# Feed-forward of a hybrid layer: two output tiles accumulated together, in two PSUM banks in turn

## The reference

```python
D_MODEL = 1024; SEQ = 2048; D_FF = 4 * D_MODEL
mix = hybrid_mixer(x, mem, ...)
x = layer_norm(alpha * x + mix, ln1_g, ln1_b)
ff = jnp.square(jax.nn.relu(x @ w_ff1)) @ w_ff2
x = layer_norm(alpha * x + ff, ln2_g, ln2_b)
```

## Time and profile before

| | |
|---|---|
| Median of 3 runs | 2450.43 us (2450.17 to 2451.43) |
| Span of the profiled execution | 2450.3 us |
| PE busy | 2343.9 us, 96% |
| DVE busy | 1361.9 us, 56% |
| ACT busy | 758.7 us, 31% |
| POOL busy | 345.0 us, 14% |
| Matmuls | 10560 |

### The profile page before, as it was taken

One profiled execution on the slowest core, in us unless ns is written; L12 is line 12 of the kernel. 1 busy time (PEld: TensorE's weight loads), 2 busy tenths in 40 slices (PEclk: granted clock), 3 DMA queues, 4 the chain that ended last, 5 costly groups with the idle time before them and its releaser, 6 DMA issues.

```text
span 2450.3 us, 29301 instructions
## 1 busy us (share of the span) xinstructions
PE 2343.9 (96%) x10560; PEld 1880.9 (77%) x10560; DVE 1361.9 (56%) x2145; ACT 758.7 (31%) x1242; POOL 345.0 (14%) x261
## 2 busy tenths in 40 slices
PE   7999999998999997999999999998999999999996
PEld 5777777777778776788888888886788888888885
DVE  4666558555846577544454454447755454454456
ACT  4434443453444344321211212215421211212213
POOL 3221112110211137200000000004720000000003
PEclk9999999999999998999999999999999999999998
DMA  6223241324132323411111111111211111111111
GB/s 182 61 58 106 61 155 35 107 66 138 49 107 69 121 90 133 155 47 50 40 51 51 34 51 51 39 47 35 93 65 49 51 51 51 34 51 51 35 51 69
DMA packets 171279, 174.17 MB, mean 71 GB/s; under 512 B 5520, under 2 KB 139696, under 8 KB 171200
## 3 DMA queue, kind: packets, MB, share of 16 engines
q1 hardware_dynamic: 160256, 134.23, 18.2%
q0 software_dynamic: 10944, 38.91, 4.3%
HBM read 156.35 MB, written 16.78 MB: 71 GB/s over the span
## 4 chain that ended last, share of the span: by engine, by line
PE 57%; DVE 5%; DMA 0%; ACT 0%; issue 0%; SPq 0%
PE main L67 9%; PE main L69 9%; PE main L68 9%; PE sc L67 5%; PE sc L68 5%; PE sc L69 5%; PE ob L67 2%; PE aux L67 2%; PE aux L69 2%; PE ob L68 2%; PE aux L68 2%; PE ob L69 2%; DVE f_xT_lo L1386 2%; DVE f_stats L1635 1%; DVE acc L1629 1%; DMA acc<-normed_dram 0%
## 5 line engine op out<-in xcount | busy, mean ns | idle before, releaser
L1629 DVE TENSOR_TENSOR acc<-acc,main 128x512 f32<-128x512 f32 x512 | 347.3, 686 | 217.1 <-PE main L69 217.1
L67 PE MATMUL main<-w_lo,h_hi 128*128 128x512 f32 x1024 | 405.8, 396 | 3.9 <-issue 2.0
L69 PE MATMUL main<-w_hi,h_hi 128*128 128x512 f32 x1024 | 404.6, 395 | 0.0
L68 PE MATMUL main<-w_hi,h_lo 128*128 128x512 f32 x1024 | 404.3, 395 | 0.0
L1553 ACT ACTIVATE w_hi<-raw 128x1024 fp32r<-128x1024 f32 x124 | 124.1, 1049 | 538.2 <-PE main L69 538.2
L1015 DVE TENSOR_TENSOR w_lo<-raw,w_hi 128x1024 fp32r<-128x1024 f32 x120 | 159.5, 1336 | 163.9 <-ACT w_hi L742 162.3
L67 PEld LDWEIGHTS main<-w_lo,h_hi 128*128 128x128 f32 x1024 | 192.7, 188 | 49.5 <-issue 2.4
L69 PEld LDWEIGHTS main<-w_hi,h_hi 128*128 128x128 f32 x1024 | 192.6, 188 | 45.6
L68 PEld LDWEIGHTS main<-w_hi,h_lo 128*128 128x128 f32 x1024 | 192.7, 188 | 45.1
L67 PE MATMUL main<-xT_lo,w_hi 128*128 128x512 f32 (+1 forms) x528 | 219.4, 416 | 1.5 <-DVE xT_lo L1027 1.5
L67 PE MATMUL sc<-f_xT_lo,w_hi 128*128 128x512 f32 x512 | 204.0, 398 | 17.3 <-DVE f_xT_lo L1386 17.3
(11 more groups left out here) (207 smaller groups left out, 3989.6 us busy)
## 6 DMA issues: line engine op xcount, KB each, us to landing
raw<-in_w_ff_dram SPq DMA_DIRECT2D x128, 512.0 KB, 4.0
raw<-in_w_in_dram SPq DMA_DIRECT2D x80, 512.0 KB, 3.8
rows<-in_x_dram POOLq DMA_DIRECT2D x32, 512.0 KB, 5.1
raw<-in_w_out_dram SPq DMA_DIRECT2D x32, 512.0 KB, 4.0
normed_dram<-rows POOLq DMA_DIRECT2D x16, 512.0 KB, 3.3
out_dram<-acc POOLq DMA_DIRECT2D x12, 512.0 KB, 3.0
acc<-normed_dram SPq DMA_DIRECT2D x8, 512.0 KB, 11.9
acc<-normed_dram POOLq DMA_DIRECT2D x8, 512.0 KB, 7.0
```

The lines of the kernel that those rows point to most:

```text
L67: pe.matmul(dst, a_hi, b_lo, start=first, stop=False)
L68: pe.matmul(dst, a_lo, b_hi, start=False, stop=False)
L69: return pe.matmul(dst, a_hi, b_hi, start=False, stop=last)
L1629: dve.tensor_tensor(dst, dst, fo[i % 4][:, :], ALU.add).then_inc(fo_free[i % 4], 1)
```

## The change

In the feed-forward, two tiles are made at once by a new function `pair`: for each step of the sum it issues high x low for both tiles, then low x high for both, then high x high for both. `hidden` pairs the two feature groups of a token group (sc0 with sc1, ob with aux), `project` the two column halves of a row group (main0 with main1, main2 with main3). `project` now takes c, and waits for both banks before the pair's first matmul. The wait for slot 1 of the weights moves ahead of the first hidden tile. In (0, 15) two transposes now stand behind each pair. The programs of ACT, DVE, POOL and SP are not changed; the ends of two tiles (`fm_done`, `fo_done`) are now signalled by two matmuls in a row.

```diff
@@ -1489,41 +1489,56 @@
     def _(pe):
         three = three_products(pe)
 
+        def pair(first, second, count):
+
+            for n in range(count):
+                pieces = [side(n) for side in (first, second)]
+                for dst, a_hi, a_lo, b_hi, b_lo in pieces:
+                    pe.matmul(dst, a_hi, b_lo, start=n == 0, stop=False)
+                for dst, a_hi, a_lo, b_hi, b_lo in pieces:
+                    pe.matmul(dst, a_lo, b_hi, start=False, stop=False)
+                done = [pe.matmul(dst, a_hi, b_hi, start=False, stop=n == count - 1)
+                        for dst, a_hi, a_lo, b_hi, b_lo in pieces]
+            return done
+
         def hidden(hf, fb):
 
-            for i in range(4):
-                f, sb_ = i % 2, i // 2
-                if i < 2:
-                    pe.wait_ge(lo_done, slot_n(hf, fb, f) + 1)
+            for sb_ in range(2):
+                if sb_ == 0:
+                    pe.wait_ge(lo_done, slot_n(hf, fb, 1) + 1)
                 pe.wait_ge(hraw_ready, h_n(hf, fb, 0))
                 tok = slice(512 * sb_, 512 * sb_ + 512)
-                for k in range(KT):
-                    col = slice(P * k, P * k + P)
-                    ins = three(fm[i][:, :], w_hi[:, f, col], w_lo[:, f, col], xT_hi[:, k, tok], xT_lo[:, k, tok],
-                                k == 0, k == KT - 1)
-                ins.then_inc(fm_done, 1)
-
-        def project(hf, fb, i):
-
-            c, d = i // 2, i % 2
-            if i == 0:
+
+                def tile(f):
+                    return lambda k: (fm[2 * sb_ + f][:, :], w_hi[:, f, P * k:P * k + P], w_lo[:, f, P * k:P * k + P],
+                                      xT_hi[:, k, tok], xT_lo[:, k, tok])
+
+                for ins in pair(tile(0), tile(1), KT):
+                    ins.then_inc(fm_done, 1)
+
+        def project(hf, fb, c):
+
+            if c == 0:
                 pe.wait_ge(lo_done, slot_n(hf, fb, 3) + 1)
-            if i % 8 == 0:
-                pe.wait_ge(h_lo_ready, h_n(hf, fb, 2 + i // 4))
-            if isinstance(fb, int) and hf == 0 and fb == 0 and i < 4:
-                pe.wait_ge(ff.main_free[i], ff.first_slot // 4)
-            pe.wait_ge(fo_free[i % 4], 4 * NFB * hf + 4 * fb + i // 4)
+            if c % 4 == 0:
+                pe.wait_ge(h_lo_ready, h_n(hf, fb, 2 + c // 2))
+            for i in (2 * c, 2 * c + 1):
+                if isinstance(fb, int) and hf == 0 and fb == 0 and i < 4:
+                    pe.wait_ge(ff.main_free[i], ff.first_slot // 4)
+                pe.wait_ge(fo_free[i % 4], 4 * NFB * hf + 4 * fb + i // 4)
             tok = slice(P * c, P * c + P)
-            for f in range(2):
-                ins = three(fo[i % 4][:, :], h_hi[:, f, tok], h_lo[:, f, tok],
-                            w_hi[:, 2 + f, 512 * d:512 * d + 512], w_lo[:, 2 + f, 512 * d:512 * d + 512],
-                            f == 0, f == 1)
-            ins.then_inc(fo_done, 1)
+
+            def tile(d):
+                return lambda f: (fo[(2 * c + d) % 4][:, :], h_hi[:, f, tok], h_lo[:, f, tok],
+                                  w_hi[:, 2 + f, 512 * d:512 * d + 512], w_lo[:, 2 + f, 512 * d:512 * d + 512])
+
+            for ins in pair(tile(0), tile(1), 2):
+                ins.then_inc(fo_done, 1)
 
         def both(hf, fb):
             hidden(hf, fb)
-            for i in range(16):
-                project(hf, fb, i)
+            for c in range(8):
+                project(hf, fb, c)
 
         pe.wait_ge(x_lo_ready, 16)
         both(0, 0)
@@ -1531,7 +1546,8 @@
             both(0, fb)
         hidden(0, NFB - 1)
         for i in range(16):
-            project(0, NFB - 1, i)
+            if i % 2 == 0:
+                project(0, NFB - 1, i // 2)
             if i == 0:
                 pe.wait_ge(hraw_ready, h_n(1, 0, 0))
             transpose_rows(pe, ff, 1, i)
```

## The result

The changed kernel takes 2483.93 us (median of 4 runs, 2478.3 to 2486.13), the kernel before 2450.3 beside it (2450.1 to 2451.43): a ratio of 1.013, 95% interval 1.0113 to 1.0148. The forecast was 2478.4 with a range of 2464 to 2488.

What follows compares the result with a forecast made beforehand. TensorE, busy 96% of the span, was taken to bound the kernel. Terms 11.8 + 2.0 + 4.5 + 7.9 + 1.8 = 28.0 us on 2450.4 gave 2478.4 us, range 2464 to 2488.

Steps and rivals of the forecast that it cites:

- part 1 (two banks in turn): All feed-forward matmuls: alternating banks, or repeating a stationary tile, leaves the 233.3 ns step unchanged; taken as 0.
- the gain of 108 or 123 us: Feed-forward steps shorten by 17.6 ns (108 us) or 20 ns (123 us); the shorter-step rival, 2355 us, had 6%.
- a loss beyond those two values: Rival: opening another bank each time lengthens feed-forward steps by 1 to 3 ns, +6 to +18 us; 4%.
- a clock that gives way: Rival: cycling through PSUM banks drops the feed-forward to the lower clock, 1229 us more, about 3680 us; 1%.
- Part 2, the chain: End of a block's first layer: two tiles ready together make the second layer's first add 1.76 us late.
- The stall: Before the second layer's third pair, TensorE waits for two adds: 0.42 us a block, bounds 0.2 to 0.65.
- (1,1): Second half's second block: the regular 0.42 us stall, plus 2.0 us because h_lo can meet POOL once.
- The start of the feed-forward: Before and in the first block (0,0): hidden tiles are late anyway, so no loss; 0.
- (0,15): Boundary between halves: later chain and one more slow x_low, 4.5 us, or 1.8 if that one escapes.
- (1,0): Second half's first block, with statistics on DVE: 6.0 us later restart plus 1.9 us lower clock, 7.9 us.
- (1,15): Last block: DVE has no slack, so its late start goes straight to the end, 1.8 us.
- The 28 stalls: All blocks but four special ones: 28 x 0.42 = 11.8 us, bounds 5.6 to 18.2.

Runs made afterwards that it cites:

- e1: Changed kernel with only the first layer's hidden tiles in pairs, the second layer tile by tile as before: 2463.77 us, ratio 1.0053.
- e2: Kernel before with only the second layer's tiles in pairs, the hidden tiles one by one: 2456.84 us, ratio 1.0026.
- e4: Changed kernel with ACT and DVE ordered by kind for a pair (both relus, both h_raw, both h_hi, both h_lo): 2463.6 us, ratio 1.005.
- e8: Changed kernel with the edits of e3, e4 and e5, and POOL and statistics arranged as in e7: 2444.81 us, ratio 0.9971.
- e3: Changed kernel with the wait for the pair's second bank moved to just ahead of the pair's second matmul: 2476.53 us, ratio 1.0104.
- e6: Kernel before with POOL's scaling of the second half's rows held back until all x_low are done: 2445.38 us, ratio 0.9968.
- e7: e6 with five of the eight statistics of block (1,0) moved behind later adds: 2439.59 us, ratio 0.9947 against the kernel before.
- e5: Changed kernel with the first two hidden tiles of the first block made one after the other, each with its own weight wait: 2481.61 us, ratio 1.0119.
- e9: The kernel of e7 run once more beside e8 on the same chip: 2442.1 us, ratio 0.9959 against the kernel before.

## Why the prediction was right, and by how much it was off

**What bounds the kernel, and part 1 (two banks in turn): right.** I had taken 0 from the equal steps of the earlier trace rows, with a bound of 0.01 us a step. e1, e2, e4 and e8 have blocks of 44.61 or 44.79 us with one layer or both in pairs, and these are the two values of the kernel before. There is neither the gain of 108 or 123 us nor a loss beyond those two values, which are 1 ns a step apart, and the granted clock was 1.00 in the regular blocks of the changed kernel, against the rival of a clock that gives way. The two matmuls in a row with the same stationary tile bring nothing either.

**Part 2, the chain: right to 0.01 us.** 1.76 late was forecast, 4.58 us after the second layer's start; it is 4.59. **The stall: right in kind, sized too low.** 0.42 was forecast, 0.48 to 0.51 is what the blocks show. The step that failed is the hand-over taken from the earlier trace rows, 0.05 us from an add's end to the waiting matmul. Here the pair of adds (1547.90, 1.28 long) ends at 1549.18 and the matmul is recorded at 1549.32, 0.14 later. The two values are not scatter. Wherever a matmul was released by an add, the delay is 0.055 us in every kernel with one bank wait ahead of it (before, e1, e3, e6, e7, e8: 13 times), and 0.146 us in every kernel with two (the changed one, e2, e4, e5: 78 times). The row of the prediction was right for one wait, and the pair has two. Why the second costs 0.09 us is open. Together with the difference between the two halves below it makes 13.4 us for the 27 blocks besides (1,1), for 11.3: 2.1 of the 4.5 us that the sum was short.

**The start of the feed-forward: set to 0.** The prediction named (0,0) and set it to 0 since its hidden tiles are late in any case. It did not follow the moved wait for slot 1 to its first use, where DVE is still at the splits. e5 shows it: 3.3 us for the wait, 1.6 given back at the second layer, and a mixer that ended 0.8 earlier in this execution, which the change can't have caused. Net 0.9.

**(0,15): 4.5 forecast, 4.2 measured**, for the stated reasons: 1.7 for the late chain (e1), 2.5 for one slow x_low more, ten for nine (e2), and e6 shows that POOL makes them slow.

**(1,0): 7.9 forecast, 8.3 measured.** The first add was to come 36.1 us into the block (1749.0 against 1712.89) and PE's restart 37.4 us into it; they came at 35.9 and 37.3 (1759.59 and 1761.03 against 1723.74). The restart is 5.8 us later against its block than before, for 6.0. From there to the end of the block it is 19.3 us, where 72 steps at full speed take 16.8: the clock cost 2.5, for 1.9. The stall itself grew by 4.9 only, since PE also came to it 0.9 us later, behind more slow steps at the block's start (12 for 7). That the first add was met to 0.2 us is in part luck. Those slow steps made the first relu 0.9 us later than forecast (13.5 us into the block against 12.6), and h_lo, which was to take 2.4 us beside POOL, took 1.11 and gave 1.3 back.

**(1,1): 2.4 forecast, 3.9 measured.** h_lo was to meet POOL once; two met it, for 0.9 us each over the undisturbed 0.69, and the stall of 2.1 us is about the forecast. What was missing is the clock: 17 matmuls where 24 fit, 1.6 us. In the kernel before idle times of 1.9 and 2.0 us had been followed by full speed, and I had taken that for granted. This 1.6 belongs to one execution: in e5, whose edit doesn't reach this block, PE idled for 2.80 us here, with full speed behind it.

**(1,15): 1.8 forecast, 1.8 measured.** DVE has no slack there, and its late start went to the end. e1, with the same late chain, loses 1.8 there as well; e2, with the early one, 0.2.

So the direction and the cause stood, and three of the five terms came out within 0.4 us (4.5, 7.9 and 1.8). The 28 stalls, 11.8, measured 13.9, and the 2.0 of (1,1) measured 3.4. The sum was 28.0 for 32.5, short by the size of the stall (2.1), the clock in (1,1) (1.5), the moved wait (0.9), and small differences. (The upper bounds of the terms add to 36.8, not 36.9.)

## What to carry to other kernels

Accumulating two tiles together doesn't change how fast TensorE goes; it changes *when* results are ready, two at once and late, and it turns four banks into two pairs. Before doing it, follow the chain behind the last pair to the first buffer that it must free, and write that chain by kind (both relus, then both products) if two tiles arrive together. Follow each moved wait to its first use as well, where the producer has no lead. And look at places where an engine off the critical path (here POOL) slows one on it: moving that work was worth more than any order of the matmuls.

## What the runs showed of the hardware that was not expected

**An undisturbed block has one of two lengths**, 44.61 or 44.79 us for 192 matmuls, that is 232.3 or 233.3 ns a step, in every kernel here. Before, the first half ran at 44.79, and the second at 44.61:

```profile
1895.02 0.40 PE L67 MATMUL sc<-f_xT_lo,w_hi 128*128 128x512 f32 x1
...
1939.62 0.39 PE L67 MATMUL sc<-f_xT_lo,w_hi 128*128 128x512 f32 x1
```

In e1 it was the other way round, and the regular blocks of e4 and e8 ran at 44.79 throughout. The value mostly changes where PE was disturbed; in one place, block (1,2) of e8 (44.69 us), it changed with no step over 0.25 us near it, some 40 us behind the last slow step. In the changed kernel, with a disturbance in each block, it changes at each of them: the second layer starts 22.40 and 22.30 us into the blocks in turn, and both halves have the same mean. That is why the same stall of 0.5 us shows as 0.41 a block in one half and 0.59 in the other. Half a kernel at one value or the other is 14 x 0.18 = 2.5 us, as much as the difference between e8 and e9. What sets the value is open.

**The clock after a short idle time is not settled by its length.** The idle time of 1.9 us in (1,0) of the kernel before was followed by full speed; in (1,1) of the changed kernel 2.0 us of idling was followed by steps at the lower level (granted clock 0.70 over 5.6 us); the waits of 6.8 and 9.8 us were followed by it too. In e5 a longer idle time at the same place was followed by full speed, 23 matmuls in 5.6 us (timeline of PE, and a stretch):

```profile
1807.17 0.70 PE L1497 MATMUL main<-w_lo,h_hi 128*128 128x512 f32 x2 [2.80 <-DVE acc L1655]
```

```profile
1807.00:1812.60 5.60, 5.43 (x23) 4.42 (x24) 4.78 (x7) 0.00 (x0) 0.00 (x0) 1.00 0.47 167
```

**Medians a few us apart say little by themselves.** The runs of the changed kernel spread over 8 us and the four of the kernel before beside them over 1.3, but beside the later runs the kernel before spread over 7 to 9 us as well (2449.21 to 2456.86 in 17 runs). Even the mixer, which no edit touches, ends between 964.63 and 968.74 us in the eleven traces. The small effects above rest on blocks and rows for that reason.
